# Attention stage of a hybrid decoder block: the second half of each merge issued in the next step, maxima by one difference and two clippings, three rounds written out

## The reference, cut to what matters

```
s = q k^T + bias;  m = max(s);  p = exp(s - m);  den = sum(p)
o_g = p v / den;   lse_g = m + log(den)
wgt = softmax over g of lse_g;   o = sum over g of wgt_g * o_g
```

## Time and profile before

| what | value |
|---|---|
| time, median of 3 runs | 1929.08 us (1924.41 to 1929.68) |
| profiled execution, its own time | 1922.07 us |
| its span | 1920.4 us |
| mean granted TensorE clock | 0.984 |
| PE busy | 1812.1 us, 94% |
| DVE busy | 1100.5 us, 57% |
| POOL busy | 874.0 us, 46% |
| ACT busy | 572.4 us, 30% |

### The profile page before, as it was taken

One profiled execution on the slowest core, in us unless ns is written; L12 is line 12 of the kernel. 1 busy time (PEld: TensorE's weight loads), 2 busy tenths in 40 slices (PEclk: granted clock), 3 DMA queues, 4 the chain that ended last, 5 costly groups with the idle time before them and its releaser, 6 DMA issues.

```text
span 1920.4 us, 24979 instructions
## 1 busy us (share of the span) xinstructions
PE 1812.1 (94%) x8628; PEld 1429.1 (74%) x8628; DVE 1100.5 (57%) x1531; ACT 572.4 (30%) x1095; POOL 874.0 (46%) x597
## 2 busy tenths in 40 slices
PE   7999899989998998999999999999999999999998
PEld 5777677767776766788788878777777777788887
DVE  5346544564645479443411232798888888944534
ACT  5532344333435333111411221533333233200000
POOL 7436442643454256554344443266555665322211
PEclk9999999989999999999999999999999999999999
DMA  4111111211020113444421134412211212145311
GB/s 165 34 39 46 49 50 39 61 40 39 28 77 33 34 35 93 112 110 117 162 89 66 66 132 153 142 66 87 78 66 66 98 66 109 55 175 189 129 44 55
DMA packets 64194, 158.09 MB, mean 82 GB/s; under 512 B 10912, under 2 KB 27680, under 8 KB 64112
## 3 DMA queue, kind: packets, MB, share of 16 engines
q1 hardware_dynamic: 51856, 145.35, 22.2%
q10 hardware_dynamic: 11792, 10.04, 1.9%
q0 software_dynamic: 464, 1.62, 0.2%
HBM read 123.54 MB, written 32.26 MB: 81 GB/s over the span
## 4 chain that ended last, share of the span: by engine, by line
PE 44%; DVE 26%; issue 18%; POOL 6%; ACT 3%; DVEq 1%; DMA 0%; POOLq 0%; SPq 0%; ACTq 0%
PE bank L887 8%; PE bank L889 7%; PE bank L888 7%; PE bank L1305 4%; PE bank L1307 4%; PE bank L1306 4%; DVE cv L1998 2%; PE bank L901 2%; PE bank L1021 2%; DVE run_z L1739 2%; PE bank L1048 2%; DVE st L1983 2%; PE bank L1035 2%; POOL wlo L627 2%; DVE gbuf L2050 2%
## 5 line engine op out<-in xcount | busy, mean ns | idle before, releaser
L887 PE MATMUL bank<-hhi,whi 128*128 128x512 f32 x1024 | 424.7, 415 | 22.9 <-DVE utmp L1702 8.5
L888 PE MATMUL bank<-hlo,whi 128*128 128x512 f32 x1024 | 407.8, 398 | 0.0
L889 PE MATMUL bank<-hhi,wlo 128*128 128x512 f32 x1024 | 407.3, 398 | 0.0
L627 POOL TENSOR_TENSOR wlo<-raw,whi 128x1024 fp32r<-128x1024 f32 (+1 forms) x84 | 196.7, 2342 | 243.3 <-DVE whi L1642 241.3
L887 PEld LDWEIGHTS bank<-hhi,whi 128*128 128x128 f32 x1024 | 195.6, 191 | 74.2 <-issue 15.6
L889 PEld LDWEIGHTS bank<-hhi,wlo 128*128 128x128 f32 x1024 | 195.2, 191 | 46.1
L888 PEld LDWEIGHTS bank<-hlo,whi 128*128 128x128 f32 x1024 | 195.8, 191 | 40.0 <-issue 1.2
L860 POOL TENSOR_TENSOR plo<-st,phi 128x512 fp32r<-128x512 f32 x60 | 108.4, 1820 | 50.2 <-ACT phi L1553 50.2
L1788 DVE CUSTOM_DVE_ANT_0 sp<-bank,mask 128x128 f32<-128x128 f32 (+1 forms) x192 | 56.3, 349 | 128.9 <-PE bank L1021 128.2
L1642 DVE CAST whi<-raw 128x1024 fp32r<-128x1024 f32 (+1 forms) x84 | 63.6, 758 | 101.9 <-PE bank L889 63.7
L1420 ACT ACTIVATE sp<-sp,negm 128x128 f32<-128x128 f32 (+1 forms) x192 | 83.9, 438 | 120.1 <-DVE negm L1792 120.1
(11 more groups left out here) (304 smaller groups left out, 4063.1 us busy)
## 6 DMA issues: line engine op xcount, KB each, us to landing
raw<-in_wblocks SPq DMA_DIRECT2D x98, 512.0 KB, 3.7
pair<-in_wblocks SPq DMA_DIRECT2D x40, 512.0 KB, 4.0
ff_scr<-ffo SPq DMA_DIRECT2D x22, 512.0 KB, 2.8
ff<-ff_scr SPq DMA_DIRECT2D x22, 512.0 KB, 4.1
rt<-rt_scr SPq DMA_DIRECT2D x8, 516.0 KB, 6.4
x<-in_xT SPq DMA_DIRECT2D x8, 512.0 KB, 8.5
zb_scr<-zb SPq DMA_DIRECT2D x8, 512.0 KB, 3.4
zb<-zb_scr SPq DMA_DIRECT2D x8, 512.0 KB, 3.3
```

The lines of the kernel that those rows point to most:

```text
L627: pool.tensor_tensor(wlo[par][:, 0:cols], raw[par][:, 0:cols], whi[par][:, 0:cols].bitcast(F32), ALU.subtract).then_inc(lo_done, 1)
L887: nc.tensor.matmul(ps, a, x, start=start and k == k_list[0], stop=False)
L888: nc.tensor.matmul(ps, a, y, start=False, stop=False)
L889: last = nc.tensor.matmul(ps, b, x, start=False, stop=stop and k == k_list[-1])
```

## The change

- The loop of three rounds is written out; `hp` is then a number, and the waits that were computed from a register are constants.
- `merge_sums` is cut in two: `merge_psum` (what reads PSUM) and `merge_z` (the update of run_z). For half 0 they come at j = 11, with `merge_psum` ahead of the last eviction of the step and `merge_z` behind `merge_max` of half 1. For half 1 they come in the next step: `merge_psum` at j = 0 behind the copy of v and the scores, `merge_z` at j = 1 behind the copy of v and the eviction. Behind step B they come in `ublock`, around the eviction of its first half. In D both halves stay in the step.
- On POOL the second half's update, normalisation and the store of `num` move into the next step's j = 0, behind a `lo`. On ACT the reciprocal of half 0 moves behind the exponential of half 1, that of half 1 to the next step's j = 1.
- `merge_max` makes up = run_n - nb, then run_n = min(run_n, nb) in place, then down = min(-up, 0) and up = min(up, 0). PSUM is free after the second instruction; a new semaphore `ab_in` tells ACT after the fourth.

```diff
-        def stage_a(eng, first, slot, ublock, enter=None, leave=None):
+        def stage_a(eng, first, slot, ublock):
             first()
-            with eng.Fori(0, HP - 1) as hp:
-                if enter:
-                    enter(hp)
+            for hp in range(HP - 1):
                 b = B_ALOOP + 10 * hp
...
@@ POOL @@
+            def rescale(ag, hp, h):
+                nm = natural(num[:, :], ag, h)
+                pool.wait_ge(ab_exp, hpc(hp, ag) + h + 1)
+                chain.link(pool.tensor_tensor(nm, nm, split2(ab[h][:, 0, :], ag), ALU.mult))
+
+            def weigh(a, ag, hp, h):
+                nm = natural(num[:, :], ag, h)
+                pool.wait_ge(d_read, 2 * a + h + 2)
+                pool.tensor_tensor(nm, nm, split2(t_num[:, h, :], ag), ALU.add).then_inc(merged, 1)
+
+            def normalise(ag, hp, h):
+                nm = natural(num[:, :], ag, h)
+                pool.wait_ge(merged, hpc(hp, ag) + h + 3)
+                pool.wait_ge(rz_done, 2 * hp + h + 1)
+                pool.tensor_tensor(nm, nm, natural(run_z[:, :], ag, h), ALU.mult).then_inc(o_ready, 1)
...
+                    if a and ag == 0 and j == 0:
+                        weigh(a - 1, 2, hp - 1, 1)
+                        normalise(2, hp - 1, 1)
+                        pool.wait_ge(o_ready, 2 * hp)
+                        pool.dma_start(o_scr[hp - 1], num[:]).then_inc(pool_dma, 16)
                     if a is not None and ag > 0 and j in (10, 11):
                         h = j - 10
...
+                        rescale(ag, hp, h)
+                        if ag == 1 or n is None or h == 0:
+                            weigh(a, ag, hp, h)
+                        if ag == 2 and n is None:
+                            normalise(ag, hp, h)
+                        elif ag == 2 and h:
+                            normalise(ag, hp, 0)
...
-                if n is not None and ag == NPAT - 1:
-                    pool.wait_ge(o_ready, 2 * hp + 2)
-                    pool.dma_start(o_scr[hp], num[:]).then_inc(pool_dma, 16)
...
@@ ACT @@
-                        act.wait_ge(m_read, 2 * a + h + 2)
+                        act.wait_ge(ab_in, 4 * hp + 2 * (ag - 1) + h + 1)
                         act.activation(ab[h][:], ab[h][:], ACT.Exp).then_inc(ab_exp, 1)
-                        if ag == NPAT - 1 and (n is not None or h == 0):
-                            reciprocal_z(hp, ag, h)
+                        if ag == NPAT - 1 and h:
+                            reciprocal_z(hp, ag, 0)
+                    if a and ag == 0 and j == 1:
+                        reciprocal_z(hp - 1, NPAT - 1, 1)
...
@@ DVE @@
             def ublock(hp, n):
-                for h in range(2):
-                    evict_u(hp, n, h)
+                a = 3 * hp + 1
+                merge_psum(a, 1, hp, 1)
+                evict_u(hp, n, 0)
+                merge_z(a, 1, hp, 1)
+                evict_u(hp, n, 1)
...
-                link(TT(new, ps, nn, ALU.min))
-                TT(split2(ab[h][:, 0, :], ag), new, nn, ALU.subtract)
-                TT(split2(ab[h][:, 1, :], ag), new, ps, ALU.subtract).then_inc(m_read, 1)
-                dve.wait_ge(m_read, 2 * a + h + 2)
-                link(V.tensor_copy(nn, new))
+                link(TT(up, nn, ps, ALU.subtract))
+                TT(nn, nn, ps, ALU.min).then_inc(m_read, 1)
+                link(V.tensor_scalar(down, up, -1.0, 0.0, ALU.mult, ALU.min))
+                V.tensor_scalar(up, up, 0.0, None, ALU.min).then_inc(ab_in, 1)
...
+                    if a and (ag < 2 or n is None) and j == 0:
+                        merge_psum(a - 1, (ag + 2) % 3, hp - (ag == 0), 1)
+                    if a is not None and j == 11:
+                        merge_psum(a, ag, hp, 0)
                     if n is not None and j % 2:
                         evict(g, b, j // 2, b_proj[j // 2 % 2])
+                    if a and (ag < 2 or n is None) and j == 1:
+                        merge_z(a - 1, (ag + 2) % 3, hp - (ag == 0), 1)
...
                     if a is not None and j >= 10:
                         merge_max(a, ag, hp, j - 10)
-                        merge_sums(a, ag, hp, j - 10)
+                    if a is not None and j == 11:
+                        merge_z(a, ag, hp, 0)
+                        if n is None:
+                            merge_psum(a, ag, hp, 1)
+                            merge_z(a, ag, hp, 1)
```

More of the change, by code:

```diff
@@ L400, in stage_a @@
                 slot(3 * hp + 3, 0, b + 7, 3 * hp + 2, 2, hp)
-            if leave:
-                leave(HP - 1)
             last = 3 * (HP - 1)
@@ L447, in load_rt @@
                                   rt_scr.rearrange("(b g) s a k -> b s g a k", g=GB)[it]).then_inc(rt_in, 16)
-            with sp_.Fori(0, HP - 1) as hp:
+            for hp in range(HP - 1):
                 for b in range(10):
@@ L797, in _ @@
             pool.sem_inc(merged, 2)
-            stage_a(pool, first, slot, ublock, lambda hp: chain.enter(hp, 47), chain.leave)
+            stage_a(pool, first, slot, ublock)
             def e1(it, last=False):
@@ L1422, in slot @@
                             last.then_inc(exp_done, 1)
-                    if a is not None and j == 8 and not isinstance(hp, int):
+                    if a is not None and j == 8 and hp < HP - 1:
                         act.dma_start(mask[ag][:], masks[ag, hp + 1]).then_inc(mask_in[ag], 16)
@@ L1426, in slot @@
                         h = j - 10
-                        act.wait_ge(m_read, 2 * a + h + 2)
+                        act.wait_ge(ab_in, 4 * hp + 2 * (ag - 1) + h + 1)
                         act.activation(ab[h][:], ab[h][:], ACT.Exp).then_inc(ab_exp, 1)
-                        if ag == NPAT - 1 and (n is not None or h == 0):
-                            reciprocal_z(hp, ag, h)
-            stage_a(act, first, slot, ublock, lambda hp: chain.enter(hp, 2), chain.leave)
+                        if ag == NPAT - 1 and h:
+                            reciprocal_z(hp, ag, 0)
+                    if a and ag == 0 and j == 1:
+                        reciprocal_z(hp - 1, NPAT - 1, 1)
+            stage_a(act, first, slot, ublock)
             def sigmoid_b(it, p, h):
@@ L1706, in ublock, with merge_psum @@
             def ublock(hp, n):
-                for h in range(2):
-                    evict_u(hp, n, h)
+                a = 3 * hp + 1
[3 more added lines that the diff above has]
+                evict_u(hp, n, 1)
             def merge_max(a, ag, hp, h):
                 dve.wait_ge(mt_done, 2 * a + h + 1)
-                nn, ps, new = natural(run_n[:, :], ag, h), split2(b_nb[:], ag), split2(t_z[:], ag)
+                nn, ps = natural(run_n[:, :], ag, h), split2(b_nb[:], ag)
                 if ag == 0:
-                    if h == 0:
-                        dve.wait_ge(pool_dma, 16 * (hp + 1))
                     V.tensor_copy(nn, ps).then_inc(m_read, 1)
                     return
+                down, up = (split2(ab[h][:, i, :], ag) for i in range(2))
                 dve.wait_ge(merged, 4 * hp + 2 * (ag - 1) + h + 1)
                 dve.wait_ge(m_read, 2 * a + h + 1)
-                link(TT(new, ps, nn, ALU.min))
-                TT(split2(ab[h][:, 0, :], ag), new, nn, ALU.subtract)
-                TT(split2(ab[h][:, 1, :], ag), new, ps, ALU.subtract).then_inc(m_read, 1)
-                dve.wait_ge(m_read, 2 * a + h + 2)
-                link(V.tensor_copy(nn, new))
-            def merge_sums(a, ag, hp, h):
+                link(TT(up, nn, ps, ALU.subtract))
+                TT(nn, nn, ps, ALU.min).then_inc(m_read, 1)
+                link(V.tensor_scalar(down, up, -1.0, 0.0, ALU.mult, ALU.min))
+                V.tensor_scalar(up, up, 0.0, None, ALU.min).then_inc(ab_in, 1)
+            def merge_psum(a, ag, hp, h):
                 nm, nz = natural(num[:, :], ag, h), natural(run_z[:, :], ag, h)
@@ L1730, in merge_sums @@
                 if ag == 0:
+                    if h == 0:
+                        dve.wait_ge(pool_dma, 16 * (hp + 1))
                     V.tensor_copy(nm, split2(b_o[h][:], ag))
@@ L1736, in merge_sums, with merge_z @@
                 TT(t_z[:], b_t[:], ab[h][:, 1, :], ALU.mult).then_inc(d_read, 1)
+            def merge_z(a, ag, hp, h):
+                if ag == 0:
+                    return
+                nz = natural(run_z[:, :], ag, h)
                 link(TT(nz, nz, split2(ab[h][:, 0, :], ag), ALU.mult))
@@ L1807, in slot @@
                         last.then_inc(stat_done, 1)
-                    if g == 2 and j == 11 and not isinstance(hp, int):
+                    if g == 2 and j == 11 and hp < HP - 1:
                         hi(b + 4, 0, need=2 * (b + 3))
@@ L1820, in slot @@
                     hi(B_E1 + 2, 0, HT, need=2 * (B_E1 + 1))
-            stage_a(dve, first, slot, ublock, lambda hp: chain.enter(hp, 28), chain.leave)
+            stage_a(dve, first, slot, ublock)
             dve.wait_ge(o_ready, 2 * HP)
```

13 lines of the change are left out of this document (2 added, 11 removed).

## The result

The changed kernel takes 1893.56 us (median of 4 runs, 1892.75 to 1894.57) against 1928.46 for the kernel before (4 runs): a ratio of 0.9826, 95% interval 0.981 to 0.9842. The forecast was 1906, range 1896 to 1921: faster, as forecast, but by some 12 us more, and outside the range. The profiled execution took 1893.21 us, its span is 1891.0 us. Two disturbed executions of some 4540 us, one of the kernel before and one in experiment 12, are left out throughout.

The account below looks back on a forecast made before the run. PE, busy 94% of the span, was taken as the bound, so only its idle time could be won: 19.8 + 0 + 0 + 3.3 = 23.1 us off the median 1929.08 gives 1906, range 1896 to 1921.

Parts of the forecast that it names:

- The base of the sum: Whole kernel: the 23.1 us won were taken from the median of 1929.08; the profiled execution took 1922.07.
- step B to ublock to step C: Start of step C, three times: between 0.6 us won and 0.7 lost each, taken as 0; POOL's `lo` holds PE.
- what lies behind stage A: The kernel after stage A: no gain forecast, 0 us.
- The last step: Last step and its end: 3.3 us won, between 1 and 5; some 2.7 of waits ahead of D.
- the changes C to A: Step C to the next step A, three times: 7.3, 7.5 and 5.0 us won, 19.8 in all.
- The third window: Third step C to A, first product to second sum of squares: 24.4 us, before 29.34.
- The clippings: DVE's two clippings in `merge_max`: 0.42 us each, bounds 0.17 and 1.07; nothing on the path to ACT's exponential.
- The second sum of squares: Third step C to A: starts at 602.0 instead of 606.98, waiting about 1 us for ACT's second square.
- PE's wait at step C's start: Sign of being right: line 887 at step C's start still 2 to 3 us late, with `lo` plainly last.
- "issue" row: PE's stops at the loop's jumps, 4.5 us in two times: gone from stage A once written out; no separate term.
- straight code that comes late: Slower rival: written-out stage A stops PE up to 2.3 us at many places; fifteen stops make 1940; chance 0.04.
- The second rival: POOL starts ahead of DVE's add in `merge_z` of half 0: 7.3 us less won, 1913; chance 0.22.

Follow-up runs that it names:

- experiment 12: Changed kernel with `lo` between rescale and weigh of half 1 on POOL: 1895.8 us; also with `merge_z`'s half 0 multiplication early: 1891.88; that multiplication alone: 1889.78.
- 5: Changed kernel with both evictions of `utmp` put back behind the whole merge of half 1 in the u block: 1893.47 us, ratio 0.983.
- 1: Kernel before with only the loop of three rounds written out: 1917.95 us, ratio 0.9955.
- 3: Changed kernel with the old four instructions for the maxima (minimum, two differences, copy behind the trigger): 1909.13 us, ratio 0.9909.
- 6: Changed kernel with a useless copy of 128x512 (`run_n` onto itself) as last instruction of `merge_max`, 16 times: 1908.46 us, ratio 0.9909.
- 7: Changed kernel with a useless copy of 128x512 (`run_n` onto itself) as last instruction of `merge_z`, 16 times: 1908.11 us, ratio 0.9911.
- 8: Changed kernel with a useless copy of 128x512 (`run_n` onto itself) as first instruction of `merge_max`, 16 times: 1909.58 us, ratio 0.9915.
- 10: Changed kernel with `merge_z`'s half 0 multiplication directly behind `merge_psum` of half 0, plus a useless copy last in `merge_max`: 1892.66 us, ratio 0.9836.

## Why the prediction was wrong where it was

**Which steps failed.** The base of the sum: 1929.08, with a trace 7 us under it that was taken to lose what the median loses (2.7 + 3.7 us of the 11.75 missing). And terms put at nothing: step B to ublock to step C (4.1 us) and what lies behind stage A (2.8). The last step was put 2.5 us too high.

**The mechanism held at the changes C to A.** The third window was forecast as 24.4 us; it is 25.2 in that trace, 23.9 and 23.5 in the two others. The clippings were put at 0.42 us and took 0.40 to 0.46. The second sum of squares, which was to wait some 1 us, has no such wait in this trace, but where the clock stays at 1.00 it waits 1.0 us at all three places, as forecast (last section). One mark went against it: PE's wait at step C's start is 0.8 us and not 2 to 3. There is no "issue" row between 60 and 800 us and no straight code that comes late (by the Trainium skill's "Runtime: NRT & Kernel Launch", section "Instruction fetch mechanics", straight code is streamed while it runs, and the trace agrees: PE has no such wait in these 740 us). Three changes C to A brought 21.1 us for 19.8 forecast, the waits ahead of D 2.6 for 2.7.

**"Step B to ublock to step C: I take 0."** The measured term is 4.1 us, past the upper end of 3 x 0.6. The releaser was named rightly, for the changed kernel (5) and, by 1, for the one before; `utmp` stood 0.8 us behind it, and the change moves that too, so a wait can shrink from 2.83 to 0.82 us. The size failed in one step: "line 774 170.5 to 172.5, first pass to 173.5, `lo` to 175.65". The weigh started at 169.99 and took 1.57 us, since no SBUF-to-SBUF instruction of DVE was under way, so that `lo` ended 1.04 us sooner, at 174.61. The duration of 2.0 that I took the earlier trace rows holds a stand of some 0.5 us: DVE's line 1737 was under way there, from 170.69 to 171.93.

**"Maxima and clippings: nothing on the path."** True of their own length, wrong as a statement on what they decide. The second rival held that race and priced it at 7.3 us; the runs in which it is lost cost 14 to 15 us more (3, 6). By ordinals in 6 they lose 2.5, 1.7 and 1.7 us at the u blocks (0.7 each was put), 1.4, 1.9 and 1.4 at the changes C to A (1.3 each), and 3 us from the last step on (1.3). That the race was won isn't what broke the forecast, which counted on it, with a margin of 0.1 us by estimates that were off by more: that it was won was in part luck, and 7.3 us understated what hung on it. The Trainium skill's rule in "SBUF — State Buffer", section "Who interferes with whom", that whoever issues first holds the shared ports for the whole instruction, agrees with experiments 3, 6, 7, 8 and 10: 1.09 or 2.25 us for the same add, 0.65 or 1.80 for the same copy.

**The last step: 3.3.** Measured 2.6 - 1.8 = 0.8. The part ahead of D was right; at D's end the two waits for `t_z` fall from 2.7 and 2.1 us to 1.7 and 0.9, but in the same stretch PE now waits 3.2 us for `olo` (0.2 before), 1.9 for `negm` and 1.3 for `w1p`, which had no wait. What comes earlier by the deferral meets the queues of DVE and ACT there; which of their instructions is in the way was not tried.

**Behind stage A: 0.** Measured 2.8 us, of which 1.5 lie at one place near 1680 us. There PE runs at 1.2 GHz in the trace of before, right behind a wait of 2.20 us:

```profile
1677.00:1679.00 2.00, 2.00 (x6) 1.63 (x5) 1.97 (x4) 0.00 (x0) 0.92 (x1) 0.50 0.35 145
```

None of the changed kernel's three traces falls to the lower level there, nor does the one of 1, but the one of 6 does. So these 1.5 us go with the execution and not with the change; the other 1.3 are open.

**"On the median: 1929.08 - 23.1."** The larger part of the miss. The sum was made on an execution of 1922.07 us and put on a median of three runs of 1929.08. Over all 54 undisturbed executions on record, the kernel before has a median of 1926.4; the base was 2.7 us high. And 1922.07 is lower than all but one of them: it lies 4.3 us under the median, where the changed kernel's three profiled executions lie on average 0.6 under theirs. So the executions of before lose 3.7 us that this trace doesn't show. The times of the executions go with the clock: the profiled execution was granted 0.984, the middle one of the 50 beside the experiments 0.981; the ten at 0.983 average 1925.5 us, the four at 0.977 1931.2. Together: 2.7 + 3.7 + 5.4 (1922.07 less the 1893.6 of the three profiled executions is 28.5, and 23.1 was forecast) = 11.8 us, against 1906 - 1894.25 = 11.75. The text named the 7 us between trace and median and then gave them no room in the range; the range's lower end had only sizes in it.

## What to carry to other kernels

Where VectorE and GpSimd meet on SBUF, read who starts first and by how much; a margin of 0.1 us is a term of the sum with a price of its own (here 14 us). Slack can be made without doing less work: one of VectorE's passes moved into an idle gap won 4 to 7 us here and took the price of a further copy from 14 us to 2. An edit can be worth -5 us alone and +15 beside another, so measure the parts in both surroundings. And when the profiled execution is several us off the median, compare the granted clocks of the two, and widen the range by that much, before anything else.

## What the runs showed of the hardware that was not expected

The granted clock differs between executions of one kernel at the same place, and the windows differ with it. The first and the third window of the changed kernel in another execution (the one of 1891.79 us), to be put beside those on top, and PE at the end of the third:

```profile
222.88:246.33 23.45, 19.30 (x95) 13.92 (x94) 18.60 (x35) 13.97 (x28) 13.82 (x9) 1.00 0.13 46
557.41:580.89 23.48, 19.29 (x95) 13.92 (x94) 18.63 (x35) 13.96 (x28) 13.84 (x9) 1.00 0.12 45
```

```profile
580.89 1.10 PE L913 MATMUL bank<-sq,cst_s 128*128 128x512 f32 x2 [1.02 <-ACT sq L1375]
```

The order is the same, and so are the waits of 0.35 to 0.4 and 2.7 to 2.8 us ahead, and the windows are 23.4, 23.8 or 25.2 us at a granted clock of 1.00, 0.93 or 0.86. From 1.00 to 0.93 only some 0.4 us are lost, because at full clock PE arrives early and waits 1.0 us for the second square; the next step costs 1.4. In the kernel before, with waits of up to 8.2 us ahead, the clock was 0.84 to 0.88 in all three windows.

Writing out the loop won 4.1 and 4.5 us at the two changes with a jump and 1.6 at the one without, while PE's own "issue" wait shows 2.24.
